# Token gather and expert-result store that skip empty slots, in a one-step Hymba/MoE kernel

## What is computed

```python
gates = gw[:, None] * ew / jnp.sum(ew, axis=-1, keepdims=True)
eid = gsel[:, None] * EXP_PER_GROUP + esel
...
hmid = jax.nn.silu(xb @ w1[e]) * (xb @ w3[e])
return hmid @ w2[e]
...
y = jnp.zeros((n + 1, d), jnp.float32).at[row_tok].add(outs * row_g[:, None])[:n]
```

## Time and profile before

| | us |
|---|---|
| median of 3 runs | 1828.31 |
| lowest, highest | 1822.43, 1830.95 |
| the profiled execution | 1825.13 |
| its span, first to last instruction | 1823.1 |

### The profile page before, as it was taken

One profiled execution on the slowest core, in us unless ns is written; L12 is line 12 of the kernel. 1 busy time (PEld: TensorE's weight loads), 2 busy tenths in 40 slices (PEclk: granted clock), 3 DMA queues, 4 the chain that ended last, 5 costly groups with the idle time before them and its releaser, 6 DMA issues.

```text
span 1823.1 us, 18498 instructions
## 1 busy us (share of the span) xinstructions
PE 1524.1 (84%) x7041; PEld 673.8 (37%) x7041; DVE 521.0 (29%) x1010; ACT 270.8 (15%) x606; POOL 56.7 (3%) x71
## 2 busy tenths in 40 slices
PE   6999989899898989959878778787878787878781
PEld 3445555565344455443222222222222222222220
DVE  3065766541213042252212111121212121212125
ACT  2113225511211032110000000000000000000001
POOL 3000000000000000000000000000000000000002
PEclk9998987779999999969998999898989999888996
DMA  8311320265841226449999999999999999999995
GB/s 285 117 47 46 117 70 1 75 222 171 306 182 58 69 107 238 159 168 405 421 423 422 423 422 422 422 422 423 422 422 422 423 422 421 422 422 422 422 389 190
DMA packets 103879, 521.45 MB, mean 286 GB/s; under 512 B 10048, under 2 KB 10608, under 8 KB 54672
## 3 DMA queue, kind: packets, MB, share of 16 engines
q1 hardware_dynamic: 85760, 468.48, 63.5%
q0 software_dynamic: 10096, 37.01, 5.7%
q10 hardware_dynamic: 7968, 15.21, 2.2%
HBM read 496.94 MB, written 23.72 MB: 286 GB/s over the span
## 4 chain that ended last, share of the span: by engine, by line
PE 43%; DMA 41%; DVE 9%; ACT 2%; SPq 2%; issue 1%; POOL 0%; ACTq 0%; DVEq 0%; POOLq 0%
DMA ring<-w 39%; PE psum L1892 10%; PE psum L2352 8%; PE psum L1880 7%; PE psum L2059 3%; PE psum L2375 2%; SPq L643 1%; PE psum L1865 1%; DVE ring L1349 1%; PE psum L1978 1%; SPq L654 1%; PE psum L2231 1%; PE psum L1997 1%; PE psum L2208 1%; DVE r_h L1218 1%
## 5 line engine op out<-in xcount | busy, mean ns | idle before, releaser
L2352 PE MATMUL psum<-ring,r_c 128*64 128x512 f32 x1536 | 405.5, 685 | 128.5 <-DMA ring<-w 127.6
L2375 PE MATMUL psum<-ring,r_c 128*64 128x512 f32 x1024 | 236.1, 599 | 52.5 <-DMA ring<-w 38.6
L2352 PEld LDWEIGHTS psum<-ring,r_c 128*64 128x64 f32 x1536 | 120.0, 157 | 410.7 <-issue 209.9
L1796 DVE TENSOR_SCALAR r_c<-r_c 128x512 f32<-128x512 f32 x32 | 13.7, 427 | 772.8 <-ACT r_c L1147 772.8
L2375 PEld LDWEIGHTS psum<-ring,r_c 128*64 128x64 f32 x1024 | 70.9, 136 | 195.6 <-issue 91.4
L1880 PE MATMUL psum<-r_h,ring 128*128 128x512 f32 x320 | 138.7, 594 | 0.0
L1892 PE MATMUL psum<-ring,r_h 128*128 128x512 f32 x256 | 116.7, 616 | 5.4 <-DMA ring<-w_in 4.2
L1147 ACT ACTIVATE r_c<-psum 128x512 f32<-128x512 f32 x32 | 19.1, 598 | 621.0 <-PE psum L2352 621.0
L1798 DVE RECIPROCAL r_c<-r_c 128x512 f32<-128x512 f32 x32 | 107.3, 3353 | 1.1
L1880 PEld LDWEIGHTS psum<-r_h,ring 128*128 128x128 f32 x320 | 60.4, 190 | 75.3 <-issue 75.3
L1892 PEld LDWEIGHTS psum<-ring,r_h 128*128 128x128 f32 x256 | 50.1, 198 | 67.1 <-issue 67.0
(11 more groups left out here) (340 smaller groups left out, 1372.0 us busy)
## 6 DMA issues: line engine op xcount, KB each, us to landing
ring<-w SPq DMA_DIRECT2D x320, 1024.0 KB, 27.1
r_h<-w SPq DMA_DIRECT2D x32, 1024.0 KB, 27.2
r_mix<-w SPq DMA_DIRECT2D x32, 1024.0 KB, 27.7
ring<-w_in SPq DMA_DIRECT2D x7, 2048.0 KB, 10.6
ring<-cache_moba_v SPq DMA_DIRECT2D x32, 256.0 KB, 4.9
ring<-cache_mem_k POOLq DMA_DIRECT2D x8, 1024.0 KB, 6.9
ring<-cache_mem_v SPq DMA_DIRECT2D x8, 1024.0 KB, 10.0
out_rows<-r_c ACTq DMA_DIRECT2D x64, 128.0 KB, 6.4
```

The costliest lines, as they stand in the source:

```text
L2352: ins = pe.matmul(psum[2 + 2 * u + m][CAP * half:CAP * (half + 1), :], xT[:, k, CAP * u:CAP * (u + 1)], moe_place(2 * q + m, u)[:, kk, 512 ...
L2375: ins = pe.matmul(psum[7][CAP * half:CAP * (half + 1), :], heT[u][:, k % 4, CAP * (k // 4):CAP * (k // 4 + 1)], ring[:, 8 + q, kk, 512 * h ...
```

## The change

- Empty slots now get an index that lies out of bounds (`NONE` = 16384 is added to the table, and token numbers in it are stored less `NONE`). The gathers have a bounds check and skip such rows; what was in `xg` stays there.
- The result of an expert leaves by one indirect DMA issued by POOL (`store_rows`), 128 rows of 2 KB, with indices `sidx` that DVE computes; rows of empty slots are skipped. ACT issues no stores any more, but for the overflow path.
- POOL's stream is now gather 0, gather 1, and then for each expert e its store, which waits for `y_free`, with gather e/2+1 ahead of the store of each even e from 2 on.
- `out_rows` is zero-filled whole: two more fills of 4 MB behind POOL's early memsets.
- A table of 128 x 64 (`c_store`) is loaded with the router's weights, and DVE has two more instructions of 128 x 32 in the router.

```diff
-    c["c_tokid"] = np.arange(5)[None] * P + p[:, None]
+    c["c_tokid"] = np.arange(5)[None] * P + p[:, None] - NONE
...
+            for k in range(NE // XBLK):
+                pool.dma_start(out_rows[XBLK * CAP * k:XBLK * CAP * (k + 1), :].rearrange("(p r) (c d) -> p (r c) d", p=P, d=P),
+                               zeros[:, :].unsqueeze(1).to_broadcast([P, n, P])).then_inc(zeros_out, 16)
...
+            pool.dma_start(store, a["c_store"]).then_inc(rtw_in, 16)
...
-                pool.indirect_dma_start(xg, None, tok_rows, bass.IndirectOffsetOnAxis(ap=table[:, c:c + 1], axis=0))\
-                    .then_inc(xg_in, 16)
-
-            for c in range(NE // 2):
-                gather(c)
+                pool.indirect_dma_start(xg, None, tok_rows, bass.IndirectOffsetOnAxis(ap=table[:, c:c + 1], axis=0),
+                                        bounds_check=TOK - 1, oob_is_err=False).then_inc(xg_in, 16)
+
+            half_rows = out_rows.rearrange("r (h c) -> (r h) c", h=2)
+
+            def store_rows(e):
+
+                pool.wait_ge(y_free, e + 1)
+                if e < 1:
+                    pool.wait_ge(zeros_out, 48)
+                    pool.wait_ge(stored_ids, 1)
+                pool.indirect_dma_start(half_rows, bass.IndirectOffsetOnAxis(ap=sidx[:, e:e + 1], axis=0), ys[e % 2], None,
+                                        bounds_check=2 * NE * CAP - 1, oob_is_err=False).then_inc(rows_in[e % 2], 16)
+
+            gather(0)
+            gather(1)
+            for e in range(NE):
+                if e % 2 == 0 and 2 <= e // 2 + 1 < NE // 2:
+                    gather(e // 2 + 1)
+                store_rows(e)
...
+                if not late:
+                    if reused(j, c):
+                        act.wait_ge(rows_in[u], 16 * (j if c >= 0 else j - 1))
+                    act.activation(ys[u], psum[7], ACT.Copy).then_inc(y_free, 1)
+                    return
...
+            v(dve.tensor_tensor(stmp, store[:, NE:2 * NE], R["cnt"], ALU.is_ge))
+            dve.scalar_tensor_tensor(out=sidx, in0=stmp, scalar=float(NONE), in1=store[:, 0:NE], op0=ALU.mult, op1=ALU.add)\
+                .then_inc(stored_ids, 1)
             J.wait_filled(dve, "table")
-            dve.tensor_copy(table[:, :], J.bank("table")[:, 0:NBLK // 2]).then_inc(routed, 1)
+            dve.tensor_scalar(table[:, :], J.bank("table")[:, 0:NBLK // 2], float(NONE), None, ALU.add).then_inc(routed, 1)
```

More of the change, by code:

```diff
@@ L47 @@
 XBLK = 16
+NONE = 1 << 14
 NBLK = NE + XBLK
@@ L90, in constants @@
     c["c_iota"] = np.broadcast_to(np.arange(P), (P, P))
-    c["c_tokid"] = np.arange(5)[None] * P + p[:, None]
+    c["c_tokid"] = np.arange(5)[None] * P + p[:, None] - NONE
+    c["c_store"] = np.concatenate([(np.arange(NE)[None] * CAP + p[:, None] % CAP) * 2 + p[:, None] // CAP,
+                                   np.broadcast_to(p[:, None] % CAP, (P, NE))], axis=1)
     c["c_steps"] = np.broadcast_to(CAP * np.arange(1, 9), (P, 8))
@@ L358, in step_kernel @@
         table = sb("table", [P, NBLK // 2], U32)
+        sidx = maskd[:, 0:NE].bitcast(U32)
+        store = maskd[:, NE:3 * NE]
+        stmp = maskd[:, 3 * NE:4 * NE]
         zeros = sb("zeros", [P, P])
@@ L496, in step_kernel @@
         onehots, routed = sem("onehots"), sem("routed")
+        stored_ids = sem("store_indices")
         out_mk, out_mv, out_s, out_mem, out_s0 = (sem(f"out_{n}") for n in ("mk", "mv", "s", "mem", "s0"))
@@ L510, in step_kernel @@
         rows_in = [sem(f"out_rows{n}_in") for n in range(2)]
+        late_in = [sem(f"late_rows{n}_in") for n in range(2)]
         moe_done, late_stored = sem("moe_done"), sem("late_stored")
@@ L759, in _ @@
             for n in range(2):
-                pool.wait_ge(rows_in[n], 32 * NE // 2)
+                pool.wait_ge(rows_in[n], 16 * NE // 2)
             for i, r in TILES:
@@ L1147, in gate_exp, with down @@
                 act.activation(he[u], psum[2 + 2 * u], ACT.Exp, scale=-1.0).then_inc(up_exp, 1)
-            def down(j, c):
+            def down(j, c, late=False):
                 u = c % 2
@@ L1153, in down @@
                 act.wait_ge(down_used, 8 * j + 4 * (c + 1))
-                if reused(j, c):
-                    act.wait_ge(rows_in[u], 32 * (j if c >= 0 else j - 1))
+                if not late:
[3 more added lines that the diff above has]
+                    return
+                act.wait_ge(rows_in[u], 16 * (NE // 2))
                 act.activation(ys[u], psum[7], ACT.Copy).then_inc(y_free, 1)
@@ L1159, in down @@
                     act.dma_start(out_rows[bass.ds(2 * CAP * j + CAP * c, CAP), 512 * half:512 * (half + 1)],
-                                  ys[u][CAP * half:CAP * (half + 1), :]).then_inc(rows_in[u], 16)
+                                  ys[u][CAP * half:CAP * (half + 1), :]).then_inc(late_in[u], 16)
             def pair(j):
@@ L1181, in _ @@
             down(NE // 2 - 1, 1)
-            act.wait_ge(zeros_out, 16)
+            act.wait_ge(zeros_out, 48)
             n_ov = act.value_load(ovi[0:1, 0:1], min_val=0, max_val=XBLK)
@@ L1189, in _ @@
                             gate_exp(j, u)
-                            down(j, u)
+                            down(j, u, late=True)
                         for u in range(2):
-                            act.wait_ge(rows_in[u], 32 * j + 32)
+                            act.wait_ge(late_in[u], 32 * j - 32 * (NE // 2 - 1))
                         act.activation(nt[0:1, 3, bass.ds(j - NE // 2, 1)], ss[0:1, 0:1], ACT.Copy).then_inc(late_stored, 1)
@@ L1661, in logit @@
                 if n == 0:
-                    dve.wait_ge(rtw_in, 64)
+                    dve.wait_ge(rtw_in, 80)
                     v(dve.memset(lg, 0.0))
@@ L2286, in logit @@
                 if n == 0:
-                    pe.wait_ge(rtw_in, 64)
+                    pe.wait_ge(rtw_in, 80)
                 J.wait_free(pe, "logit", i)
```

## The result

The changed kernel takes 1815.84 us (median of 20 runs, 1811.18 to 1825.36); the kernel before took 1825.23 in the 20 runs beside it. The ratio is 0.9946 [0.9936, 0.9957]: 0.54% faster, some 9.4 us, against the 9.0 of the prediction. (The time of 1819.3 was reckoned from 1828.31, the median of before that was at hand; that is 3.1 us above the runs beside this one and makes most of the distance.) The profiled execution took 1812.56 us with a span of 1810.4, so it is 12.7 us shorter than the profiled one of before (1823.1).

What follows compares the result with a forecast made beforehand. DMA work was taken to bound the expert stage, half of the run. The terms summed to -9.6 + 0.6 = -9.0 us, so 1828.3 - 9.0 = 1819.3 us, range 1807 to 1831.

Steps and rivals of the forecast that it cites:

- Term 1: Expert stage, gathers and stores: skipping 46.9% of rows gives -9.6 us, the middle between 0 and 19.3.
- The rival that all of it counts: Expert stage: engines take partitions in turn or share one limit, -19.3 us, 1809.6 in all; chance 0.22.
- The rival that nothing comes back: Expert stage: fullest engine loses no rows, or skipped rows cost about as much as moved; 1828.9 us; chance 0.16.
- Dearer scattered rows: Expert-stage stores: a row costs k times before, 1819.3 + 16 (k - 1) us, gain gone at 1.6; chance 0.11.
- The late gather: Gathers behind stores on POOL: landing over 18 us stalls PE, beyond some 40 costs time, 1834 and more; chance 0.03.
- Term 2: Expert stage: stores issued by POOL instead of ACT, same bytes in the queues; cost 0.
- Term 4: Span's end: the last result leaves by POOL's scatter; 4.4 - 3.7 = +0.6 us, between -1 and +2.
- Term 5: Router: two added DVE operations of 128x32 fit in DVE's idle wait for PE; cost 0, without cover 0.45 us.
- Term 6: Early span: two 4 MB zero fills beside the third weight load; cost 0, or 2 to 7 us if served after them.
- Two of the signs: Expert stage: DMA share below 1.01 means one engine paces, 1.01 even load; packet number as before means nothing skipped.

Runs made afterwards that it cites:

- the first two experiments: Kernel after with only the order of an expert's 64 slots changed: the even order, 1812.63 us, and the lumped order, 1824.39 us.
- the even order: Kernel after with filled slots spread over the groups of four partitions, same rows moved; 1812.63 us, ratio 0.9923; repeated 1811.54 us, 0.9913.
- the third experiment: Kernel after with nothing skipped: empty slots gather row 0, all 64 rows of each expert scattered by POOL; 1829.67 us, ratio 1.0018.
- the lumped order: Kernel after with eight ranks in a row filling one group of four partitions and the group 32 further on; 1824.39 us, ratio 0.9993.

## Why the prediction was right

The mechanism of the main term was right, its size was a guess that came out near, and in the sum two misses cancel. Against before, the stage gained 11.6 us where 9.6 was forecast (10.4 by skipping, 1.1 by the moved stores), and the end cost 2.2 where 0.6 was. That the whole time came within half a microsecond of the forecast difference is in part luck.

**Term 1, skipped rows: -9.6 forecast, -10.4 measured** (the stage, against the one with no slot skipped). The reason given was the right one: a weight chunk is waited for as a whole, so the fullest engine sets the pace, and the layout of the empty slots decides how much comes back. Moving them alone swings the stage by 12.9 us. The number had less behind it than the reason: 9.6 was the middle between 0 and 19.3, and it came out near because slots in order lie about midway, which no row of before could tell: luck. The Trainium skill's map, put there beside it, gave 9.2. By the runs it is the better base, since it gives the order of three layouts, though it is off by 1 to 2.5 us in each.

**The rival that all of it counts** (1809.6) falls with the first two experiments: under a common limit the order of slots would be of no account, and with partitions dealt in turn the kernel after would have been ahead of the even one. **The rival that nothing comes back** falls with the third. **Dearer scattered rows**: with no row skipped all 21.0 us of stores count, and k = 1.6 would have made that stage 12.6 us longer than before. It is 1.1 shorter, so k is 1 or a little under. **The late gather** fell too. The last result's copy and the last gather after (timeline):

```profile
1676.43 0.60 ACT L1184 ACTIVATE r_c<-psum 128x512 f32<-128x512 f32 x1 [8.32 <-PE psum L2409]
```
```profile
1677.82 0.98 POOL L771 DMA_INDIRECT out_rows<-r_c,maskd  x1 [29.26 <-ACT r_c L1184]
1679.11 1.05 POOL L760 DMA_INDIRECT r_c<-tok_rows,table  x1 [0.30 <-issue]
```
```profile
1697.68 1.22 PE L2368 MATMUL psum<-ident,r_c 128*128 128x128 f32 x8
```

From issue to use there are 18.6 us, and no gather took over 9.2 to land. So the cover is 9.4 us or more, where 3.5 to 10 was forecast. The line's own view (ns least, median, most) and who waited for it:

```profile
L760 POOL DMA_INDIRECT r_c<-tok_rows,table x16: 1008/1042/1065, 810.8 to 1679.1; - x16
...
  PE psum L2368: 5.2, 1
...
DMA to landing us min/median/max: 4.0/8.8/9.2
```

PE waited once, for the first gather, as before.

**Term 2, stores by POOL: 0 forecast**, and the third experiment bears it out. The stores' own line:

```profile
L771 POOL DMA_INDIRECT out_rows<-r_c,maskd x32: 971/986/1027, 858.8 to 1771.4; - x32
its engine sat idle before it (us, times) until:
  ACT r_c L1184: 873.9, 31
```

They were issued in 971 to 1027 ns each, and the gathers' 1008 to 1065 is some 0.1 us over the earlier trace rows. The Trainium skill's "DVE blocks DMA" trap (SBUF — State Buffer, section "SBUF: two separate sides") would show as issues or landings held up for longer. Neither is seen (a gather landed in 9.2 us at most, against 10.0 before), but this kernel doesn't test it: in its trace DVE stands idle during all 48 of these issues. Before, DVE was at work during 15 of the 16 gather issues (14 times with L1798, a RECIPROCAL of 128x512), and none took over 1.01 us; whether that is an operation of the kind that the trap names, no run here shows.

**Term 4, the end: +0.6 forecast, +2.2 measured; the one step that failed.** The price was right: the indirect store landed in 4.31 us, and 4.4 had been taken. The subtraction was wrong (and 4.4 - 3.7 is 0.7, not 0.6). 3.74 was the whole gap of the earlier trace rows, from the copy's end to the next gather, and it holds 0.54 before the transfer and 0.82 behind it. The 4.4 was a landing alone. Like with like is 4.3 - 2.4 = +1.9; another 0.25 goes by until POOL has begun its issue (0.79 us after the copy's end, where ACT's transfer began after 0.54).

**Term 5, the router: 0, and right.** DVE after:

```profile
808.42 0.19 DVE L1815 TENSOR_TENSOR maskd<-maskd,r_mix 128x32 f32<-128x32 f32 x1
808.64 0.19 DVE L1816 SCALAR_TENSOR_TENSOR maskd<-maskd 128x32 uint32<-128x32 f32 x1
809.75 0.18 DVE L1819 TENSOR_SCALAR table<-psum 128x24 uint32<-128x24 f32 x1 [0.92 <-PE psum L2351]
```

The two new operations are taken out of DVE's idle time: 1.44 us before, 0.92 now.

**Term 6, the zeros: 0, and right.** PE's third stretch on `w_in`, at 83.95 in the earlier trace rows, starts at 82.73 without a wait. DMA is busy 87% of the first 60 us against 72% before, and the weight load issued beside the fills took 17.2 us to land against 11.5, where 20 to 25 was forecast:

```profile
82.73 27.73 PE L1914 MATMUL psum<-r_h,ring 128*128 128x512 f32 x64
```
```profile
0.00:60.00 60.00, 46.11 (x248) 24.56 (x249) 13.84 (x41) 16.44 (x32) 17.63 (x25) 1.00 0.87 300
```

What it would cost to leave the added fills out was not tried.

**Two of the signs were badly chosen.** The text said that a DMA share below 1.01 would show one engine as the pace, and a share of 1.01 an even load. It stayed at 1.01 with an uneven load, which fits engines with fewer rows drawing on weights queued ahead, some 27 us of them by their landing. Only in the lumped order does the rate dip, late, and even there the share over the 640 us is 1.01; it falls only at the stage's very end. The text also said that a number of packets as before would mean that nothing is skipped. The page's lines, before and after:

```profile
DMA packets 103879, 521.45 MB, mean 286 GB/s; under 512 B 10048, under 2 KB 10608, under 8 KB 54672
```
```profile
DMA packets 103431, 522.02 MB, mean 288 GB/s; under 512 B 11490, under 2 KB 12050, under 8 KB 54224
```

## What to carry to other kernels

Where 16 DMA engines share every transfer and the consumer waits for whole transfers, count the work of the fullest engine and not the mean. If rows are to be skipped, deal the empty ones over the partitions so that each engine loses its share; here two tables of constants were worth nearly 5 us more of stage. When one operation replaces another on the critical path, compare the same piece of it, issue to landing with issue to landing, and add the starts on both sides separately. And judge such a change by the length of its own stage, which repeated to 0.1 and 0.5 us, where whole times scattered by 10. A mean DMA share doesn't show an uneven load: it read 1.01 in the even and in the lumped order alike.

## What was not expected of the hardware

- A row that an indirect DMA skips still leaves a packet: 1906 small ones more, with the total unchanged at 103431; 961 of them appear when the gathers alone skip and 947 when the stores alone do, where two rows of 2 KB share a packet. They cost little, since the even order gave back 15 of the 19.3 us that all rows together would be worth.
- An uneven load stays hidden for long: the lumped order ran at the full rate of some 421 GB/s for 567 us of the stage before its rate dipped.
- The lumped order still gave 2.5 us, though by the Trainium skill's map its fullest engine loses no row. Faster packets account for little of it: leaving out those over 0.5 us, the weight queue's packets of 8192 bytes took 312.6 ns on average from 1384 to 1720 us, against 313.5 in the even order, which is 0.3%, some 1 us over that stretch (an estimate). The rest stays open.
- At the end of the experts an indirect store of one expert's rows (2 KB each) landed in 2.74 to 4.38 us, and two plain ones in 2.38 and 2.39. Skipping isn't what makes it slow: with whole stores the landing was 4.29 us (nothing skipped) and 2.93 (only the gathers skip).
